# A transformer encoder layer on one core: the order of work at its start, in its routing stage and at its end

## The chip, the cores and the metric

One core of a Trainium2 chip runs the whole layer as one program, float32 throughout except for small bfloat16 index and mask tables. The metric is the device time of one execution in microseconds. The kernel before takes 2204.61 us (median of 3 runs, 2203.73 to 2205.79). Engines: TensorE (PE, its weight loads PEld), VectorE (DVE), ScalarE (ACT), GpSimd (POOL), SyncE (SP), which only issues DMAs.

## The reference, cut to what matters

1024 tokens of width 1024, one layer, in float32:

```
h    = rmsnorm(x, norm1);  proj = h @ w_in            # 1024 x 2048: q, k, v, pool
att  = diff_attention(q, k, v, rel_table, lambda)     # 4 heads, T5 bias by distance
pool = pool_mixer(p, w_pool, pool_scale)              # windows 2, 4, 8, 16
x    = x + concat(att, pool) @ w_out
h    = rmsnorm(x, norm2);  logits = h @ w_router + b_router
topv, topi = top_k(logits, 4);  gates = softmax(topv)  # 4 of 32 experts
# each expert on its own tokens:
#   g = min(h@w_gate+b_gate, 7);  u = clip(h@w_up+b_up, -7, 7)
#   y = ((u+1) * g * sigmoid(1.702 g)) @ w_down + b_down, times its gate
out  = rmsnorm(x + sum of the gated y, final_norm)
```

rmsnorm scales each token by the inverse root of the mean of its squares, then by a gain per channel.

## The kernel before, in words

The code holds one instruction stream per engine, written out by hand; semaphores are the only order between them, and within an engine or a DMA queue everything goes in program order. A DMA adds 16 to its semaphore. Tokens are in eight tiles of 128.

**Start (0 to 220 us).** SyncE loads token tiles 0 to 3, the pool columns of `w_in` (8 loads of 256 KB, semaphores `s_w[k]`), the q, k, v columns (8 loads of 768 KB, one semaphore `s_wqkv`, L457), the relative-bias table, its one-hot matrix and the edge factors (L460, `s_small`), four lambda vectors, and token tiles 4 to 7 (L464). For each tile ScalarE sums the squares (`square_tokens`, L775), GpSimd makes the inverse root (L583, L584), VectorE scales the tile (`scale_tokens`, L1015) into one of two buffers, TensorE transposes it in eight 128x128 blocks (`transposes`, L1413), and VectorE moves them with the gain into `hT` (`move_hT`, L1021, two moves a tile). The projection is done by a Winograd form of Strassen's scheme in eight column pairs: `half_product` multiplies half of the inner dimension (4 steps k) of one block. `first_products(n)` makes the two first products of pair n from tokens 0 to 511 (tiles 0 to 3) (L1427; from pair 6 on L1423). ScalarE moves the first (`move_first`, L780), VectorE adds the second (`sum_first`, L1029). Pairs 0 and 1 run interleaved by k, each product 512 tokens wide. Then come four small products that make the bias rows of the heads (L1449), which VectorE moves out of PSUM bank 0 (`bias_and_lambda`, L995, ahead of the factor lambda, L999 to L1005, of which ScalarE makes the exponential, L787); ScalarE stores them (L789) and SyncE repeats them in DRAM. TensorE goes on with pairs 2 to 7; after pairs 3 and 4 it transposes tiles 4, 5 and 6, 7. Those of tile 4 also wait for the bias rows to have left bank 0. A program record of a float32 product is two MATMUL records in the trace.

**Attention and output projection (220 to 505 us)** are not touched. Expert 0's `w_gate` is loaded meanwhile.

**Routing (to 545 us).** Over turns i, software-pipelined: VectorE adds the residual of tile i, normalises tile i-1, scales the gates of tile i-3 (`finish_gates`, L1169, L1170) and finds the top 4 of tile i-2 (`top_k`, L1153 to L1164); ScalarE squares, stores normed rows to DRAM (`store_rows`, L853), takes the exponential of the gates of i-3 (`gate_exp`, L868), moves the router's parts of i-2 (`move_logits`, L874) and the transposes of i-1 (`move_h2T`, L863). TensorE then ranks tokens per expert (L1622); VectorE finds the slots, compares (L1223) and builds the tables of work items (L1250 to L1279). An item is up to 128 tokens of one expert. GpSimd gathers an item's rows from DRAM (`gather_rows`, L685) after all normed rows are stored. TensorE finds row numbers (`first_rows`, L1638), transposes gathered rows (`row_transposes`, L1656), and makes the index products (L1649). Expert 0's `w_up` (L493, waits for the stored normed rows) and `w_down` (L500, waits for the first gather) are loaded by SyncE.

**Items (to 2187 us).** For each item: gate and up products (L1717, L1730), activation, transposes (L1738), down products (L1765, L1776, L1788, L1800). The rows of item j+1 are gathered while j runs. Results are added to DRAM rows by indirect DMAs (L729). The weights of the next expert are loaded as TensorE has used the last.

**End.** During the last item the residual rows come back; ScalarE sums their squares (`square_rows`, L928), GpSimd makes the inverse roots for tiles 0 and 1, 2 and 3, then 4 to 7 at once (L748, L749), VectorE scales them (L1372), SyncE stores them. Then VectorE takes up the last item's result (L1378), whose rows are normed and scattered to the output by themselves (to L756).

Of the kernel before, what the change touches and what calls it, by code (L numbers as in the profile page):

```python
# [30 lines left out]
P = 128  # L31
# [33 lines left out]
def encoder_kernel(nc, t, out):  # L65

    with ExitStack() as ctx:
# [181 lines left out]
        s_wqkv = sem("w_qkv_in")  # L249
        s_grows = sem("gain_rows_in")  # L250
        s_small = sem("small_in")
        s_ident = sem("ident_ready")
# [13 lines left out]
        s_xs = sem("xs_ready")  # L266
        s_xtr = sem("xs_transposed")
# [99 lines left out]
        s_one = sem("last_item_one_ready")  # L367
# [81 lines left out]
        def _(sp):  # L449
# [6 lines left out]
            for k in range(DT):  # L456
                sp.dma_start(w_qkv[:, k, :], wd[k][:, 0:3 * HALF]).then_inc(s_wqkv, 16)  # L457
# [108 lines left out]
        def _(pl):  # L566
            step = [0]

            def link(ins):
# [6 lines left out]
                             pattern=[[-1, P]], channel_multiplier=1).then_inc(s_ident, 1)  # L576
# [3 lines left out]
            pl.wait_ge(s_const, 3)  # L580
# [11 lines left out]
            def weight_sums(n):  # L592
# [5 lines left out]
                if n == 2:  # L598
                    pl.wait_ge(s_wqkv, 16 * DT)
# [140 lines left out]
            pl.memset(lsq[:, UNIT:UNIT + 1], 1.0).then_inc(s_one, 1)  # L740
# [5 lines left out]
            for lo, hi in ((0, 2), (2, 4), (4, 8)):  # L746
# [16 lines left out]
        def _(act):  # L763
# [18 lines left out]
            for i in range(4):  # L782
                square_tokens(i)
            for n in range(2):
                move_first(n)
            act.wait_ge(s_lamd, 2)
            act.activation(lame, lamd, ACT.Exp).then_inc(s_lame, 1)  # L787
            act.wait_ge(s_bvec, 4)
            act.dma_start(bvec_d[:, :], bvec).then_inc(s_bvout, 16)  # L789
            for i in range(4, TT):  # L790
                square_tokens(i)
            act.wait_ge(s_bps, 4)
            for n in range(2, PAIRS):
                move_first(n)
# [81 lines left out]
            for i in range(TT + 2):  # L876
# [101 lines left out]
        def _(dve):  # L978
# [13 lines left out]
            def bias_and_lambda():  # L992
                for c in range(4):
                    dve.wait_ge(s_bps, c + 1)
                    dve.tensor_copy(bvec[:, c * HALF:(c + 1) * HALF],  # L995
                                    PS[32 * c:32 * c + HEADS, 0:HALF]).then_inc(s_bvec, 1)
                dve.wait_ge(s_lamin, 64)
# [197 lines left out]
            for i in range(TT + 2):  # L1195
# [820 lines left out]
```

## Time and profile before

| what | value |
|---|---|
| median of 3 runs | 2204.61 us |
| profiled execution, its own time | 2207.8 us |
| its span | 2206.0 us |
| TensorE busy | 2133.9 us (97%) |
| VectorE, ScalarE, GpSimd busy | 676.1, 615.0, 506.0 us |
| mean granted TensorE clock | 0.985 of full |
| DMA | 500.71 MB, mean 227 GB/s |

TensorE does nearly all that lies on the chain. Of the forty slices of the page the granted clock is 9 tenths or more in all but one, which holds the routing stage (7 tenths).

### The profile page before, as it was taken

Reading aid. Unit: us, or ns where it says so; the run is one execution under the profiler, and the core shown is the slowest. Engines: PE = TensorE matmul, PEld = TensorE weight load, DVE = VectorE, ACT = ScalarE, POOL = GpSimd, SP = SyncE. Lnnn points to the kernel's source line nnn. Section 1 sums busy time; section 2 is a strip of 40 time slices with the busy share of each in tenths; the row PEclk is TensorE's granted clock in tenths of the full one; section 3 lists DMA queues with packets and bytes.
Section 4 is the critical chain, followed back from the end, with each engine's and each line's share of the span. In section 5 each row is a group of like instructions: output and inputs, shape, how many; then the busy total and the mean of one; then the engine's idle time right before and its main releaser. Section 6 shows DMA issues by size and latency. Waiting matters only on the chain.

```text
span 2206.0 us, 30272 instructions
## 1 busy us (share of the span) xinstructions
PE 2133.9 (97%) x10160; PEld 997.1 (45%) x10161; DVE 676.1 (31%) x1911; ACT 615.0 (28%) x1200; POOL 506.0 (23%) x519
## 2 busy tenths in 40 slices
PE   7999999996999999999998999999999999999996
PEld 3547676543444344344343434434443444444443
DVE  3322898245231221211222212212112211222123
ACT  2000887112222332222223222222222222222223
POOL 3172112123211222121122121221112121222222
PEclk9999999997999999999999999999999999999998
DMA  8000200425758878668869696794889868677775
GB/s 313 0 36 7 111 1 2 154 99 223 245 170 330 295 256 270 251 239 293 329 231 352 233 347 214 242 324 151 330 312 370 338 241 291 240 255 266 260 267 190
DMA packets 150746, 500.71 MB, mean 227 GB/s; under 512 B 10553, under 2 KB 35918, under 8 KB 150158
## 3 DMA queue, kind: packets, MB, share of 16 engines
q1 hardware_dynamic: 115040, 444.81, 52.6%
q0 software_dynamic: 33792, 50.35, 11.1%
q10 hardware_dynamic: 1874, 5.02, 0.6%
q8 instruction: 24, 0.39, 0.1%
q14 instruction: 16, 0.13, 0.0%
HBM read 461.26 MB, written 43.09 MB: 229 GB/s over the span
## 4 chain that ended last, share of the span: by engine, by line
PE 93%; DMA 4%; DVE 1%; issue 1%; SPq 1%; ACT 0%; POOL 0%; DVEq 0%; ACTq 0%; POOLq 0%
PE psum L1730 42%; PE psum L1765 14%; PE psum L1427 6%; PE psum L1528 5%; PE psum L1776 5%; PE psum L1551 3%; PE psum L1517 3%; PE psum L1423 2%; PE psum L1656 2%; PE psum L1717 2%; DMA weights<-in_w_down 2%; PE psum L1738 2%; PE psum L1800 1%; PE psum L1788 1%; PE psum L1560 1%; DMA weights<-in_w_up 1%
## 5 line engine op out<-in xcount | busy, mean ns | idle before, releaser
L1730 PE MATMUL psum<-weights,work 128*128 128x512 f32 (+2 forms) x3008 | 950.1, 595 | 3.4 <-DMA weights<-in_w_up 3.4
L1730 PEld LDWEIGHTS psum<-weights,work 128*128 128x128 f32 (+2 forms) x3008 | 366.7, 159 | 518.8 <-issue 517.5
L729 POOL DMA_INDIRECT residual_rows<-work x184 | 286.8, 1559 | 530.7 <-ACT work L947 480.0
L1765 PE MATMUL psum<-weights,work 128*128 128x512 f32 x768 | 337.5, 592 | 0.0
L1240 DVE SCALAR_TENSOR_TENSOR work<-psum,work 128x4 f32<-128x4 f32 x47 | 7.6, 163 | 841.7 <-PE psum L1649 841.7
L685 POOL DMA_INDIRECT work<-normed_rows,work x48 | 55.3, 1152 | 755.8 <-PE psum L1656 581.3
L1765 PEld LDWEIGHTS psum<-weights,work 128*128 128x128 f32 x768 | 142.2, 190 | 160.7 <-issue 160.7
L917 ACT ACTIVATE work<-psum 128x256 f32<-128x256 f32 x188 | 72.0, 383 | 420.2 <-PE psum L1730 391.6
L1306 DVE TENSOR_SCALAR work<-psum 128x256 f32<-128x256 f32 x188 | 79.8, 424 | 291.3 <-ACT work L917 291.1
L947 ACT ACTIVATE work<-psum,work 128x256 f32<-128x256 f32 x184 | 72.2, 475 | 321.5 <-PE psum L1765 229.5
L897 ACT ACTIVATE work<-psum 128x512 f32<-128x512 f32 x96 | 57.6, 600 | 342.4 <-PE psum L1656 341.9
L1528 PE MATMUL psum<-weights 128*128 128x512 f32 x256 | 112.7, 594 | 0.0
L1776 PE MATMUL psum<-weights,work 128*64 128x512 f32 x480 | 109.6, 598 | 0.0
L1427 PE MATMUL psum<-weights 128*128 128x512 f32 x240 | 107.8, 606 | 1.3 <-DVE weights L1021 1.3
L921 ACT ACTIVATE work<-psum 128x256 f32<-128x256 f32 x188 | 72.5, 386 | 129.5 <-PE psum L1738 129.5
L1311 DVE SCALAR_TENSOR_TENSOR work<-work 128x256 f32<-128x256 f32 x188 | 80.0, 426 | 19.5
L1105 DVE CUSTOM_DVE_ANT_0 work<-psum,weights 128x1024 f32<-128x1024 f32 x64 | 78.4, 1225 | 11.6 <-PE psum L1517 11.4
L812 ACT ACTIVATE work<-work,negmax 128x1024 f32<-128x1024 f32 x64 | 73.3, 1145 | 22.2 <-DVE negmax L1109 22.2
L1308 DVE TENSOR_TENSOR work<-psum,work 128x256 f32<-128x256 f32 x188 | 78.0, 415 | 0.0
L1427 PEld LDWEIGHTS psum<-weights 128*128 128x128 f32 x240 | 46.4, 195 | 60.1 <-issue 58.6
L1717 PE MATMUL psum<-weights,work 128*32 128x256 f32 x1024 | 64.1, 407 | 8.2 <-DMA weights<-in_w_up 6.7
L1528 PEld LDWEIGHTS psum<-weights 128*128 128x128 f32 x256 | 47.4, 190 | 54.1 <-issue 54.1
(236 smaller groups left out, 1856.3 us busy)
## 6 DMA issues: line engine op xcount, KB each, us to landing
weights<-in_w_gate SPq DMA_DIRECT2D x64, 2048.0 KB, 7.9
weights<-in_w_up SPq DMA_DIRECT2D x64, 2048.0 KB, 12.5
weights<-in_w_down SPq DMA_DIRECT2D x64, 2048.0 KB, 11.4
weights<-in_w_in SPq DMA_DIRECT2D x8, 768.0 KB, 14.2
residual_rows<-x SPq DMA_DIRECT2D x9, 512.0 KB, 3.8
normed_rows<-work ACTq DMA_DIRECT2D x9, 512.0 KB, 3.9
x<-in_x SPq DMA_DIRECT2D x8, 512.0 KB, 9.6
bias_rows_repeated<-bias_rows SPq DMA_DIRECT2D x4, 1024.0 KB, 9.8
```

Of the source, the lines that this page charges most:

```text
L729: pl.indirect_dma_start(acc_d[:, :], bass.IndirectOffsetOnAxis(dest[:, b:b + 1], 0), yrow[:, b * BLK:(b + 1) * BLK], None, compute_op=ALU. ...
L812: act.activation(pr, pr, ACT.Exp, bias=negmax[:, c:c + 1], accum_out=expsum[:, c:c + 1]).then_inc(s_ex, 1)
L1105: dve.tensor_tensor_reduce(out=prob[:, set_of(u), m, :], in0=PS[:, 2 * m * HALF:(2 * m + 2) * HALF], in1=bias[:, h, at:at + SEQ], scale=1. ...
L1306: dve.tensor_scalar(ucl[:, b, :], bank(b, BLK, BLK), LIMIT + 1.0, 1.0 - LIMIT, ALU.min, ALU.max).then_inc(s_ucl, 1)
L1308: dve.tensor_tensor(gact[:, b, :], bank(b, BLK), sig[:, b, :], ALU.mult).then_inc(s_sg, 1)
L1311: dve.scalar_tensor_tensor(hid[:, b, :], gact[:, b, :], ACT_LIMIT, ucl[:, b, :], ALU.min, ALU.mult).then_inc(s_hid, 1)
L1427: mm = pe.matmul(bank(b), w[:, k, :], a[:, k, :], start=k == 0, stop=k == 3)
L1528: mm = pe.matmul(bank(n % 4), mixT[:, c, i * P:(i + 1) * P], w_out[:, c, q * HALF:(q + 1) * HALF], start=(c == 0), stop=(c == DT - 1))
L1717: mm = pe.matmul(out, xT[:, k, 0:32], wgu[:, :, k, at:at + P], start=(k == 0), stop=(k == DT - 1))
L1730: mm = pe.matmul(out.rearrange("p (m n) -> p m n", m=2), xT[:, k, lo:lo + cols], wgu[:, :, k, blk * BLK:(blk + 1) * BLK], start=(k == 0), ...
L1765: mm = pe.matmul(bank(4 + h), actT[:, k, :], wdn[:, k, h * HALF:(h + 1) * HALF], start=False, stop=(k == DT - 1))
L1776: mm = pe.matmul(PS[64 * h:64 * h + 64, 4 * HALF:5 * HALF], actT[:, 2 * b + s, 64 * c:64 * c + 64], wdn[:, k, h * HALF:(h + 1) * HALF], st ...
```

## The change

Four places, told in the order of the streams.

1. Start. `w_qkv`'s second four loads get their own semaphore, and pair 2's second product waits for it. ScalarE scales tiles 2 and 3 with the inverse root. TensorE's first products of pairs 0 and 1 run on token columns 0 to 255 (tiles 0, 1) and then on 256 to 511; tile 3 is transposed after step k=1. The bias-row products come after pair 2. ScalarE squares tiles 4 to 7 right after moving pairs 0 and 1. VectorE scales tiles 4 and 5, makes the factor, sums pair 2, and then moves the bias rows.
2. Routing. Order of ScalarE's and VectorE's last turns; SyncE's loads of `w_up` and `w_down` of expert 0 no longer wait for the stored rows and the gather; TensorE transposes the gathered rows ahead of its register loads and the second `first_rows`.
3. End. Inverse roots in pairs of tiles.
4. Two semaphores are merged into others.

```diff
 # SyncE
-                sp.dma_start(w_qkv[:, k, :], wd[k][:, 0:3 * HALF]).then_inc(s_wqkv, 16)
+                sp.dma_start(w_qkv[:, k, :], wd[k][:, 0:3 * HALF]).then_inc(s_wqkv if k < 4 else s_wqkv_hi, 16)
             sp.wait_ge(s_y1, 2 * TT)
-            for b in range(2):
-                sp.wait_ge(s_xnout[b], 16 * TT // 2 + 16 * (1 - b))
             for half in range(2):
                 load_gu(1, half, 0)
-            sp.wait_ge(s_xg, 16)
             for half in range(2):
                 load_dn(half, 0)
 # GpSimd
-            pl.memset(lsq[:, UNIT:UNIT + 1], 1.0).then_inc(s_one, 1)
+            pl.memset(lsq[:, UNIT:UNIT + 1], 1.0).then_inc(s_lsq, 1)
-            for lo, hi in ((0, 2), (2, 4), (4, 8)):
+            for lo, hi in ((0, 2), (2, 4), (4, 6), (6, 8)):
 # ScalarE, start
             for i in range(4):
                 square_tokens(i)
+            for i in range(2, 4):
+                act.wait_ge(s_rstd, i + 1)
+                act.wait_ge(s_xtr, 2 * i - 2)
+                act.activation(xs[:, i % 2, :], xv[:, i, :], ACT.Copy, scale=rstd[:, i:i + 1]).then_inc(s_xs_act, 1)
             for n in range(2):
                 move_first(n)
+            for i in range(4, TT):
+                square_tokens(i)
             act.wait_ge(s_lamd, 2)
             act.activation(lame, lamd, ACT.Exp).then_inc(s_lame, 1)
+            move_first(2)
             act.wait_ge(s_bvec, 4)
             act.dma_start(bvec_d[:, :], bvec).then_inc(s_bvout, 16)
-            for i in range(4, TT):
-                square_tokens(i)
             act.wait_ge(s_bps, 4)
-            for n in range(2, PAIRS):
+            for n in range(3, PAIRS):
                 move_first(n)
 # ScalarE, routing
-                if i >= 3:
+                if 3 <= i < TT:
                     gate_exp(i - 3)
                 if i >= 2:
                     move_logits(i - 2)
                 if 1 <= i <= TT:
                     move_h2T(i - 1)
+                if i >= TT:
+                    gate_exp(i - 3)
 # VectorE, start (bias_and_lambda is split into move_bias_rows and difference_factor)
             scale_tokens(0)
+            scale_tokens(1)
             for i in range(4):
-                if i < 3:
-                    scale_tokens(i + 1)
                 move_hT(i)
             sum_first(0)
             sum_first(1)
-            bias_and_lambda()
-            sum_first(2)
             scale_tokens(4)
             scale_tokens(5)
+            difference_factor()
+            sum_first(2)
+            move_bias_rows()
             sum_first(3)
 # VectorE, routing
-                if i >= 3:
+                if 3 <= i < TT:
                     finish_gates(i - 3)
                 if i >= 2:
                     top_k(i - 2)
+                if i == TT:
+                    finish_gates(TT - 3)
...
             compare(pick0)
+            finish_gates(TT - 2)
             finish_gates(TT - 1)
 # TensorE, start
-            for i in range(4):
+            for i in range(3):
                 transposes(i)
-            pe.wait_ge(s_hT, 8)
-            for k in range(DT):
-                pe.wait_ge(s_w[k], 16)
-                for n in range(2):
-                    mm = half_product(n, ("A11", "A12")[k // 4], ("B11", "B21")[k // 4], 4 + 2 * n + k // 4, ks=[k % 4])
-                    if k % 4 == 3:
-                        mm.then_inc(s_proj, 1)
-            pe.wait_ge(s_small, 16 * N_SMALL)
-            for c in range(4):
-                pe.matmul(PS[32 * c:32 * c + HEADS, 0:HALF], reltab, onehot[:, c * HALF:(c + 1) * HALF],
-                          start=True, stop=True).then_inc(s_bps, 1)
-            pe.wait_ge(s_wqkv, 16 * DT)
+            for half in range(2):
+                pe.wait_ge(s_hT, 4 * half + 4)
+                for k in range(DT):
+                    if half == 0:
+                        pe.wait_ge(s_w[k], 16)
+                    for n in range(2):
+                        mm = half_product(n, ("A11", "A12")[k // 4], ("B11", "B21")[k // 4], 4 + 2 * n + k // 4, [k % 4],
+                                          slice(half * 2 * P, (half + 1) * 2 * P))
+                        if half == 1 and k % 4 == 3:
+                            mm.then_inc(s_proj, 1)
+                    if half == 0 and k == 1:
+                        transposes(3)
             for n in range(2, PAIRS):
+                if n == 2:
+                    pe.wait_ge(s_wqkv, 16 * 4)
                 first_products(n)      # its second product waits for s_wqkv_hi when n == 2
+                if n == 2:
+                    pe.wait_ge(s_small, 16 * N_SMALL)
+                    for c in range(4):
+                        pe.matmul(PS[32 * c:32 * c + HEADS, 0:HALF], reltab, onehot[:, c * HALF:(c + 1) * HALF],
+                                  start=True, stop=True).then_inc(s_bps, 1)
 # TensorE, routing, after the product of the item tables
+            pe.wait_ge(s_xg, 16)
+            row_transposes(0)
             pe.wait_ge(s_tab, 3)
             second = pe.value_load(items[0:1, 1:2], min_val=0, max_val=EXPERTS - 1)
             n_items = pe.value_load(total[0:1, 0:1], min_val=EXPERTS, max_val=MAX_ITEMS)
-            pe.wait_ge(s_xg, 16)
-            row_transposes(0)
-            first_rows(1, bass.ds(second, 1), pickT, second_rows_out)
-            pe.wait_ge(s_xT, 1)
-            row_transposes(1)
-            pe.wait_ge(s_parts, TT)
...
+            # the register loads of the first item, before behind index(1), now stand here
+            pe.wait_ge(s_xT, 1)
+            row_transposes(1)
+            first_rows(1, bass.ds(second, 1), pickT, second_rows_out)
+            pe.wait_ge(s_parts, TT)
```

## Rows read from the trace of the kernel before

**Rows 1.** The page's part 4, first line: share of each engine.
```profile
PE 93%; DMA 4%; DVE 1%; issue 1%; SPq 1%; ACT 0%; POOL 0%; DVEq 0%; ACTq 0%; POOLq 0%
```

**Rows 2.** Timeline to 100 us: start, duration, engine, line, operation, count [idle before <-releaser].
```profile
8.23 4.85 PE L1413 MATMUL psum<-ident,work 128*128 128x128 f32 x24 [1.12 <-DVE work L1015]
...
15.89 14.00 PE L1427 MATMUL psum<-weights 128*128 128x512 f32 x32 [1.30 <-DVE weights L1021]
...
21.04 6.51 SPq L464 DMA_DIRECT2D x<-in_x  x4
...
32.40 1.47 PE L1449 MATMUL psum<-work 32*4 32x512 f32 x8 [2.50 <-DMA edge<-in_edges]
...
33.80 16.91 PE L1427 MATMUL psum<-weights 128*128 128x512 f32 x32
33.87 2.83 DVE L995 COPY work<-psum 4x512 f32<-4x512 f32 x4 [3.18 <-PE psum L1449]
...
41.12 1.06 ACT L775 ACTIVATE work<-x 128x1024 f32<-128x1024 f32 x1
...
67.78 13.98 PE L1423 MATMUL psum<-weights 128*128 128x256 f32 x64
```

**Rows 3.** One source line's transfers, from issue to landing: L457, then L464.
```profile
DMA to landing us min/median/max: 9.6/14.2/19.9
...
DMA to landing us min/median/max: 12.1/12.6/13.2
```

**Rows 4.** Stretches, start and attention: length, busy of five engines, PEclk, DMA share, GB/s.
```profile
30.00:32.00 2.00, 0.00 (x0) 0.00 (x0) 0.69 (x1) 0.00 (x0) 0.00 (x0) 1.00 1.01 166
...
39.00:40.00 1.00, 1.00 (x3) 0.51 (x2) 0.00 (x0) 0.91 (x3) 0.58 (x2) 0.65 0.00 0
...
230.00:235.00 5.00, 3.33 (x17) 1.54 (x16) 3.84 (x7) 4.12 (x9) 0.00 (x0) 1.00 1.02 410
```

**Rows 5.** Timeline of the routing stage, 512 to 550 us.
```profile
512.73 0.94 SPq L493 DMA_DIRECT2D weights<-in_w_up  x2
...
512.79 0.19 DVE L1153 TENSOR_TENSOR work<-psum,work 128x32 f32<-128x32 f32 x1
...
515.90 0.19 DVE L1153 TENSOR_TENSOR work<-psum,work 128x32 f32<-128x32 f32 x1 [0.43 <-PE psum L1597]
...
522.40 1.23 POOL L685 DMA_INDIRECT work<-normed_rows,work  x1 [3.89 <-issue]
...
528.14 0.92 SPq L500 DMA_DIRECT2D weights<-in_w_down  x2
...
529.66 1.11 PE L1656 MATMUL psum<-ident,work 128*128 128x128 f32 x4 [2.30 <-issue]
...
534.19 0.98 POOL L685 DMA_INDIRECT work<-normed_rows,work  x1 [4.34 <-PE psum L1656]
...
535.34 4.97 PE L1717 MATMUL psum<-weights,work 128*32 128x256 f32 x64 [1.51 <-issue]
...
543.23 0.65 PE L1656 MATMUL psum<-ident,work 128*128 128x128 f32 x4 [2.93 <-DMA work<-normed_rows,work]
...
544.59 5.35 PE L1717 MATMUL psum<-weights,work 128*32 128x256 f32 x64
```

**Rows 6.** Source line L685 (gathers of an item's rows), issue to landing.
```profile
DMA to landing us min/median/max: 4.2/7.8/8.9
```

**Rows 7.** Timeline of the last items and the end.
```profile
2134.53 3.66 PE L1717 MATMUL psum<-weights,work 128*32 128x256 f32 x64
...
2177.44 10.46 PE L1765 MATMUL psum<-weights,work 128*128 128x512 f32 x24
2177.62 0.69 POOL L749 TENSOR_TENSOR weights<-weights,halfneg 128x2 f32<-128x2 f32 x1
...
2182.86 0.20 POOL L748 TENSOR_SCALAR weights<-weights 128x4 f32<-128x4 f32 x1 [4.55 <-ACT weights L928]
...
2184.26 4.87 DVE L1372 SCALAR_TENSOR_TENSOR x<-x,weights,work 128x1024 f32<-128x1024 f32 x4 [3.43 <-POOL weights L749]
```

More of the change, by code:

```diff
@@ L266, in encoder_kernel @@
         s_xs = sem("xs_ready")
+        s_xs_act = sem("xs_ready_act")
         s_xtr = sem("xs_transposed")
@@ L579, in _ @@
             pl.memset(pT[:, :, PAD + SEQ:], 0.0).then_inc(s_const, 1)
-            pl.wait_ge(s_const, 3)
+            pl.wait_ge(s_const, 4)
             def rsqrt_mean(dst, src, n, scratch):
@@ L598, in weight_sums @@
                 if n == 2:
-                    pl.wait_ge(s_wqkv, 16 * DT)
+                    pl.wait_ge(s_wqkv, 16 * 4)
+                    pl.wait_ge(s_wqkv_hi, 16 * 4)
                 if n >= 2:
@@ L996, in bias_and_lambda, with difference_factor @@
                                     PS[32 * c:32 * c + HEADS, 0:HALF]).then_inc(s_bvec, 1)
+            def difference_factor():
                 dve.wait_ge(s_lamin, 64)
@@ L1394, in _ @@
         def _(pe):
-            pe.wait_ge(s_ident, 1)
+            pe.wait_ge(s_const, 4)
             pe.wait_ge(s_grows, 64)
@@ L1401, in transposes @@
             def transposes(i):
-                pe.wait_ge(s_xs, i + 1)
+                if 2 <= i < 4:
+                    pe.wait_ge(s_xs_act, i - 1)
+                else:
+                    pe.wait_ge(s_xs, i + 1 if i < 2 else i - 1)
                 if i == 0:
@@ L1414, in transposes, with half_product @@
                     mm.then_inc(s_xtr, 1)
-            def half_product(n, tokens, weights, b, ks=range(4)):
+            def half_product(n, tokens, weights, b, ks=range(4), cols=slice(0, HALF)):
                 a, w = tok_blk[tokens], wgt_blk(n, weights)
@@ L1426, in half_product @@
                 for k in ks:
-                    mm = pe.matmul(bank(b), w[:, k, :], a[:, k, :], start=k == 0, stop=k == 3)
+                    mm = pe.matmul(bank(b)[:, cols], w[:, k, :], a[:, k, cols], start=k == 0, stop=k == 3)
                 return mm
@@ L1433, in first_products @@
                 half_product(n, "A11", "B11", 4 + 2 * (n % 2)).then_inc(s_proj, 1)
+                if n == 2:
+                    pe.wait_ge(s_wqkv_hi, 16 * 4)
                 if n >= 2:
@@ L1667, in _ @@
             n_items = pe.value_load(total[0:1, 0:1], min_val=EXPERTS, max_val=MAX_ITEMS)
-            pe.wait_ge(s_xg, 16)
-            row_transposes(0)
-            first_rows(1, bass.ds(second, 1), pickT, second_rows_out)
-            pe.wait_ge(s_xT, 1)
-            row_transposes(1)
-            pe.wait_ge(s_parts, TT)
-            pe.wait_ge(s_sel, 1)
-            pe.wait_ge(s_idx, 1)
-            index(0, parts_e[:, 0, :, :], pick0)
-            index(1, at=4)
             next_tokens = pe.alloc_register("next_tokens")
@@ L1685, in _ @@
             pe.reg_load(third_expert, items[0:1, 2:3])
+            pe.wait_ge(s_xT, 1)
+            row_transposes(1)
+            first_rows(1, bass.ds(second, 1), pickT, second_rows_out)
+            pe.wait_ge(s_parts, TT)
+            pe.wait_ge(s_sel, 1)
+            pe.wait_ge(s_idx, 1)
+            index(0, parts_e[:, 0, :, :], pick0)
+            index(1, at=4)
             def rows_of(b):
@@ L1956, in _ @@
             pe.wait_ge(s_glast, 32)
[L1957 to L1958 removed]
+            pe.wait_ge(s_lsq, 1 + UNIT)
             for n, lhs in enumerate((ident[:, :], same[:, 0, :], same[:, 1, :])):
```

10 lines of the change are left out of this document (4 added, 6 removed).

## The prediction

> **What bounds the kernel now.** Page first: TensorE is busy 97% of the span, and of the chain that ended last 93% is its work [rows 1], so time is to be had only where TensorE stands still, runs at the lower clock, or has ended. I read the clock slices of the page, TensorE's waits, and then the timelines of the three places that the diff touches. The reader is to see:
>
> Start. TensorE transposes three token tiles until 13.08 us, waits for the fourth and its move, and starts the first products only at 15.89; they end at 29.9; it stands 2.5 us for a small transfer, does the bias-row products, and goes on at 33.8 [rows 2]. These 2.5 us cost more: the granted clock, full (2.4 GHz) at 30 to 32 us, falls to half behind the hole and rises only within 39 to 40, where the mean is 0.65 [rows 4], so the next 32 records (pairs 2 and 3) take 16.91 us where the first 32 took 14.00 [rows 2].
>
> Routing, 505 to 545 us. A chain on VectorE with short steps of the others; TensorE is idle or at the lower clock; the last wait is the second gather of rows, 534.19 to 543.1 [rows 5].
>
> End. TensorE's last product streams to 2187.9, but VectorE takes it up only at 2189.1, since its four last row scalings began at 2184.26, after one wait for four square sums [rows 7].
>
> Between these, TensorE has no wait that the diff touches: an earlier start is passed on one to one. The three stalls on expert weights later are of loads that TensorE's own progress releases, so they move along.
>
> **Start.** The order becomes: transposes of tiles 0, 1, 2; products on token columns 0 to 255 with the transposes of tile 3 after k=1; columns 256 to 511; pair 2; bias-row products; pair 3; and so on.
> Scaling of tiles 2 and 3 goes from VectorE (0.75 us each) to ScalarE (about 1.1, as its squares of the same 128x1024). ScalarE ends its fourth square at 10.4 and so delivers tile 2 at 11.5, as VectorE did. The third tile's transposes still end near 13.0 (they are the last 8 of the first 24 [rows 2]). VectorE has one scaling less ahead of its moves of tile 1, which then end near 12.4. Products start at 13.0 in place of 15.9.
> Weights: the eight small loads land 7.6 to 8.3 us after issue, the last at 15; k=7 is wanted at 19.8: no wait. Each product is cut in two of half width: 64 records in place of 32. The records of 256 columns in a later stretch (64 in 13.98 us [rows 2]) take 0.218 us each; the 128x128 weight loads take 0.19 and hide. So 14.0 us of products plus 0.9 us for tile 3's eight transposes: end at 27.8.
> Pair 2, first product: 8 records, 3.4 us, to 31.2. It needs the first four of the large loads, issued until 9.4 and landed by 23 (median 14.2 us after issue). The other four end with the last at 10.99+19.9=30.9 [rows 3]: no wait, or tenths. Second product to 34.6. Bias rows: their last input was there at 32.4 [rows 2]; 1.47 us at half clock, 0.8 at full: 35.4. Pair 3: 6.9 us, to 42.3, against 50.7 before. That would be 8.4 us.
> It is not all kept, because of what now stands before the next transposes: they wait for the four moved bias rows (same PSUM bank). VectorE moves these after the difference factor and the sum of pair 2; the factor waits for ScalarE's exponential, which is now queued behind the squares of tiles 4 to 7. Tile 7's load is the fourth at 21.04 and after, issued about 26.9, landing 12.1 later = 39.0 [rows 2, 3]. Square (1.06 [rows 2]) with its read, 1.25: 40.3; exponential and factor 0.7: 41.0; sum of pair 2: 41.8; four moves 2.83 [rows 2]: 44.7. TensorE stands 2.4 us and does the transposes at 44.8 in place of 50.6: gain 5.8 us. The bias rows' store lands near 47 instead of 39; its first reader is VectorE's first token sum, over 20 us behind the store before, and the loads made from it are wanted far later still.
> Does this stall drop the clock? Bounds: 1.67 us of idle in 230 to 235 left it at 1.00 [rows 4]; the 2.5 us at 30 dropped it, for 16.91-13.8=3.1 us, and the 2.9 us before 543.2 did too, for 5.35-3.66=1.7 [rows 5, 7]. In those places little but idle surrounds it or small products follow; here full-size products stand on both sides. I take no drop, gain 5.8; bounds 2.7 and 8.4.
> The merged semaphores (identity, the constant one), the split weight wait and GpSimd's order of waits cost nothing: each was signalled microseconds before its reader.
>
> **Routing.** In the last two turns the move of logits and of transposed rows goes ahead of the gates' exponentials, and VectorE's top-4 ahead of the gate scalings. Before, tile 6's logits waited on ScalarE for an exponential that waited for tile 5's top-4; VectorE then stood until 512.79 [rows 5]. Now they are moved near 510.1; top-4 of tile 6 starts when that of tile 5 ends (511.8) and takes 1.9, to 513.7. One gate scaling (0.4), then tile 7's at 514.1 against 515.90 [rows 5]: 1.8 us. After the first comparison there are now two gate scalings, 0.4 more, of which 0.1 to 0.2 falls into VectorE's wait for the row products: 0.3 back. So the tables and both index chains are 1.5 us early.
> The loads: w_up (4 MB) is issued at 507 rather than 512.7 and w_down (4 MB) right behind it rather than at 528.1, when the first gather had landed [rows 5]. At the 0.41 MB/us of the stretch they and the stores fill the DMA engines until about 532. So the first gather, issued at 520.9, meets them all the way. It took 5.7 us before with half its time free; gathers span 4.2 to 8.9 [rows 6], and the one under the w_down load took 8.9. I take 8.2: landed 529.1, against 528.1.
> TensorE's first transposes were held until 529.66 by the register loads behind the tables; now they stand ahead of them: 529.2 to 530.3. Then five register loads instead of two (2 us, from the 1.5 us that two took), the second transposes at 532.4, the second row product to 534.4, the second gather's issue 1.9 later: 536.2, later than 534.19. But the DMA is free by then: 4.4 us, 540.6. TensorE starts item 0's first half near 535.9 (register loads already done; 535.34 before), ends it in 4.97 at 540.8, and goes on at once: 540.8 for 543.2, 2.4 us. With no 2.9 us hole the clock stays up: 64 records in 3.66 instead of 5.35 [rows 5, 7], 1.7. Together 4.1. Bounds: if the first gather takes 5.7 it lands at 526.6, everything is ready 2.4 us sooner: 6.5. If the gather's contention and the moved register loads cost all that the order gives: 0; below that, the rival.
> The normed rows' last store (509.8) has 11 us until the gather needs it; it took 3.
> GpSimd's parts of the gates are done before the first gather as before (518.5), and the four further ones of the last two tiles end at 528, ahead of the second.
>
> What the loads do to a gather shows as 8.9 us in full traffic, 4.2 free. The Trainium skill (DMA: Bandwidth & Descriptors, Queues, rings and completion order) says that each DMA engine alternates between the queues that have work, packet by packet, whichever engine issued it. Worked out from that rule, and so an estimate: the 0.5 MB of a gather would lose only its own length once more, 1.2 us, and land near 526.5; the routing sum by it would be that of rival 2. The 4.7 us between free and full [rows 6] are more than the rule allows, so the trace does not agree, and the sum goes by the rows.
>
> **End.** The square sums of tiles 4, 5 are there at 2180.3 (one square and its read, 1.24 each, before the last two), of 6, 7 at 2182.8. A pair costs GpSimd about 1.1 (0.2, a gap, 0.69 for the power of 128x2), four cost 1.4 [rows 7]. VectorE's tiles 4 and 5 run 2181.5 to 2183.9, tiles 6 and 7 2183.95 to 2186.4: 2.7 us earlier than 2189.1. What is late next is the last product: 2187.9. Gain 1.15 us. Bounds: 0 (were the product's real end later) and 2.7.
>
> **Sum.** 5.8+4.1+1.1=11.0 us. The profiled execution took 2207.8 (span 2206.0); 2196.8. The median shown is 3.2 below it: 2193.6.
>
> **Rivals.**
> 1. The stall at 42 us drops the clock: 1.7 to 3.1 back, 2196.0. For it: a hole of 2.5 did so at 30. Against: 1.67 did not.
> 2. The first gather is as quick as before: 2191.2. For: separate queues. Against: the 8.9.
> 3. Half-width products pay for their weight loads: 32 more loads; if 0.1 to 0.19 us of each shows, the first products end 3 to 6 us later and the 2.4 us stall takes the first of it: 0.6 to 3.6 lost, 2196.5 at 0.165 each. For: a load (0.19) nearly fills the 0.218. Against: that later stretch runs at this pace.
> 4. Routing gives nothing and the clock drops: 2.7+0+1.1=3.8, 2200.8: no change.
> 5. Slower: the 8 MB drain ahead of what is behind them. 8/0.41=20 us from 507: the last normed rows land at 530, the first gather (8.9) at 539, the second is issued near 546 and lands at 550.5 or, at 8.9, 555: 12 us later than 543.1, less 1.7 of clock, less 6.9 of start and end: +3.4; with rival 1 too +5.8, 2210. It decides once the second gather lands later than about 551.7. For: w_down no longer waits for the gather, which looks like a guard. Against: the gather under w_down still took only 8.9.
>
> **Chances.** Forecast 0.40 (own range 2191.5 to 2195.5), rival 1 0.22, rival 2 0.12, rival 3 0.10, rival 4 0.10, rival 5 0.06. About 0.2% (4.4 us) is what a measurement of this kernel tells from none. Faster: 0.84; same 0.10 (rival 4); slower 0.06. Range 2188.5 to 2200.5: from a routing gain of 6.5 with the whole 8.4 of the start to just past rival 4's edge.
>
> **What would show it.** First products from 13.0; second product of pair 2 near 31 without a wait; a wait of TensorE on the moved bias rows of 2 to 3 us near 42 and clock 1.00 behind it (or not: rival 1); tile 7's top-4 at 1.8 us less; first gather landing in 8 us; no hole before the second gather's transposes; last row scaling 2.7 us before its old time. Wrong if TensorE waits for w_in at 16 to 31 us, if the gap at 42 is over 5 us, or if item 0 starts later than before by over 3 us.

## The result and the profile after

The changed kernel takes 2240.3 us (median of 4 runs) against 2204.2 us before (4 runs): ratio 1.0167, 95% interval 1.0149 to 1.0186. It is 36 us slower; forecast were 11 us less. The profiled execution took 2243.7 us, its span is 2241.9.

The page of the changed kernel; of part 3 the last row but one is the queue that brings instructions (number, MB, share). Its part 4 answers to [rows 1]:
```profile
span 2241.9 us, 30339 instructions
...
q8 instruction: 60, 0.98, 0.2%
...
PE 92%; DMA 4%; issue 2%; DVE 1%; SPq 0%; POOL 0%; ACT 0%; DVEq 0%; ACTq 0%; POOLq 0%
...
L1752 PE MATMUL psum<-weights,work 128*128 128x512 f32 (+2 forms) x3008 | 961.2, 602 | 33.8 <-issue 29.9
...
L1739 PE MATMUL psum<-weights,work 128*32 128x256 f32 x1024 | 66.4, 415 | 17.3 <-issue 9.5
```
And the rows of the page before that answer to them, none of which the prediction looked at:
```profile
q8 instruction: 24, 0.39, 0.1%
...
L1730 PE MATMUL psum<-weights,work 128*128 128x512 f32 (+2 forms) x3008 | 950.1, 595 | 3.4 <-DMA weights<-in_w_up 3.4
...
L1717 PE MATMUL psum<-weights,work 128*32 128x256 f32 x1024 | 64.1, 407 | 8.2 <-DMA weights<-in_w_up 6.7
```
L1752 and L1739 are the gate and up products of the items, L1730 and L1717 before; no line of theirs was edited. They now wait 29.9 and 9.5 us on "issue", that is on nothing that the profile shows, and are busy 11.1 and 2.3 us longer. The instruction queue made 60 transfers instead of 24.

**The edited stages did nearly what was forecast.** TensorE's timeline of the start, after, with VectorE's moves of the bias rows (DVE; answers to [rows 2]):
```profile
12.71 1.89 PE L1440 MATMUL psum<-weights 128*128 128x256 f32 x8
...
15.31 15.69 PE L1440 MATMUL psum<-weights 128*128 128x256 f32 x64
...
33.14 3.70 PE L1440 MATMUL psum<-weights 128*128 128x512 f32 x8 [2.15 <-DMA weights<-in_w_in]
36.77 1.04 PE L1474 MATMUL psum<-work 32*4 32x512 f32 x8
37.74 7.13 PE L1440 MATMUL psum<-weights 128*128 128x512 f32 x16
...
42.32 2.82 DVE L1000 COPY work<-psum 4x512 f32<-4x512 f32 x4
...
45.24 1.94 PE L1426 MATMUL psum<-ident,work 128*128 128x128 f32 x16 [0.37 <-issue]
```
First products from 12.71 (forecast 13.0), the next transposes at 45.24 (44.8). But the stall is elsewhere: 2.15 us on `w_in` at 31, and 0.37 instead of 2.4 ahead of those transposes.

Routing, after (answers to [rows 5]):
```profile
515.42 1.22 POOL L683 DMA_INDIRECT work<-normed_rows,work  x1 [1.33 <-issue]
...
523.18 1.12 PE L1678 MATMUL psum<-ident,work 128*128 128x128 f32 x4 [2.80 <-DMA work<-normed_rows,work]
...
528.40 0.98 POOL L683 DMA_INDIRECT work<-normed_rows,work  x1 [5.55 <-DVE work L1242]
529.06 5.64 PE L1739 MATMUL psum<-weights,work 128*32 128x256 f32 x64 [0.75 <-issue]
534.71 0.65 PE L1678 MATMUL psum<-ident,work 128*128 128x128 f32 x4
```
The first gather is used 7.8 us after its issue (8.2 forecast), the second at most 6.3; the hole of 2.93 us before the second transposes is gone. The second item's products begin at 544.70, against 554.87 before: 10.2 us ahead, where 5.8 + 4.1 were forecast. At the end the last product waits for nothing that scales rows (answers to [rows 7]):
```profile
2215.05 10.46 PE L1787 MATMUL psum<-weights,work 128*128 128x512 f32 x24
...
2222.43 2.48 DVE L1382 SCALAR_TENSOR_TENSOR x<-x,weights,work 128x1024 f32<-128x1024 f32 x2 [0.58 <-POOL weights L747]
2225.55 1.66 DVE L1388 SCALAR_TENSOR_TENSOR work<-psum,work,weights 128x256 f32<-128x256 f32 x4 [0.64 <-PE psum L1787]
```

**All of the loss lies in the items.** From the first product of the second item to the start of the last product of all: 1632.4 us before, 1680.2 after, 47.8 more. TensorE's timeline where a 96-token item ends (L1810 is its last line) and a 32-token one begins, after:
```profile
733.15 3.66 PE L1810 MATMUL psum<-weights,work 128*32 128x256 f32 x64
742.44 1.49 PE L1739 MATMUL psum<-weights,work 128*32 128x256 f32 x9 [5.63 <-issue]
747.06 5.43 PE L1739 MATMUL psum<-weights,work 128*32 128x256 f32 x55 [3.14 <-issue]
```
Stretches of it; the columns are those of [rows 4], and the third number from the end is PEclk, the granted share of the full clock:
```profile
730.00:737.00 7.00, 6.81 (x80) 2.84 (x76) 0.23 (x1) 0.88 (x4) 0.00 (x0) 1.00 1.02 413
737.00:750.00 13.00, 4.42 (x37) 2.19 (x41) 0.00 (x0) 3.93 (x6) 6.23 (x4) 0.67 1.05 372
...
742.00:744.00 2.00, 1.49 (x9) 0.56 (x10) 0.00 (x0) 0.00 (x0) 1.69 (x2) 0.50 1.02 406
```
Before, the 64 products there took 3.66 us in one piece; now 9 of them come after a hole of 5.63 us, and the other 55 after one of 3.14. The granted clock is 1.00 until the hole, 0.50 behind it at 742 to 744, and 0.67 on average from 737 to 750.

The kept trace also has the start of each transfer of the instruction queue. Before, the last of the 24 starts at 733.6 us. After, two start in the first of these holes, at 737.1 and 738.9, and one in the second, at 744.8. The changed kernel has eight waits on issue of over 1 us among its items: in seven of them at least one such transfer starts, and the eighth, of 1.79 us, begins as one ends.

### The profile page after: what moved, and what is told of

The parts are those of the page before. It is cut to its first block, busy times and chain, and to the rows that moved or that the text cites. A ratio compares the mean times of both kernels' runs of the same rounds, so it can differ in the third digit from the quotient of the medians.

```text
span 2241.9 us, 30339 instructions
## 1 busy us (share of the span) xinstructions
PE 2141.1 (96%) x10192; PEld 1003.7 (45%) x10193; DVE 673.1 (30%) x1909; ACT 617.0 (28%) x1202; POOL 510.3 (23%) x521
## 4 chain that ended last, share of the span: by engine, by line
PE 92%; DMA 4%; issue 2%; DVE 1%; SPq 0%; POOL 0%; ACT 0%; DVEq 0%; ACTq 0%; POOLq 0%
PE psum L1752 42%; PE psum L1787 15%; PE psum L1440 6%; PE psum L1550 5%; PE psum L1798 4%; PE psum L1573 3%; PE psum L1539 3%; PE psum L1739 2%; PE psum L1436 2%; PE psum L1678 2%; PE psum L1760 2%; DMA weights<-in_w_down 2%; PE psum L1810 1%; PE psum L1822 1%; PE psum L1582 1%
## 5 line engine op out<-in xcount | busy, mean ns | idle before, releaser
L1752 PE MATMUL psum<-weights,work 128*128 128x512 f32 (+2 forms) x3008 | 961.2, 602 | 33.8 <-issue 29.9
L1752 PEld LDWEIGHTS psum<-weights,work 128*128 128x128 f32 (+2 forms) x3008 | 369.6, 161 | 557.4 <-issue 554.3
L1550 PE MATMUL psum<-weights 128*128 128x512 f32 x256 | 112.7, 594 | 0.0
L1798 PE MATMUL psum<-weights,work 128*64 128x512 f32 x480 | 109.6, 598 | 0.0
L1440 PE MATMUL psum<-weights 128*128 128x512 f32 (+1 forms) x272 | 105.3, 543 | 2.1 <-DMA weights<-in_w_in 2.1
L1739 PE MATMUL psum<-weights,work 128*32 128x256 f32 x1024 | 66.4, 415 | 17.3 <-issue 9.5
L1440 PEld LDWEIGHTS psum<-weights 128*128 128x128 f32 x272 | 51.2, 190 | 52.8 <-issue 48.2
L1550 PEld LDWEIGHTS psum<-weights 128*128 128x128 f32 x256 | 47.4, 190 | 54.1 <-issue 54.1
```

The source lines that it names most:

```text
L1440: mm = pe.matmul(bank(b)[:, cols], w[:, k, :], a[:, k, cols], start=k == 0, stop=k == 3)
L1550: mm = pe.matmul(bank(n % 4), mixT[:, c, i * P:(i + 1) * P], w_out[:, c, q * HALF:(q + 1) * HALF], start=(c == 0), stop=(c == DT - 1))
L1739: mm = pe.matmul(out, xT[:, k, 0:32], wgu[:, :, k, at:at + P], start=(k == 0), stop=(k == DT - 1))
L1752: mm = pe.matmul(out.rearrange("p (m n) -> p m n", m=2), xT[:, k, lo:lo + cols], wgu[:, :, k, blk * BLK:(blk + 1) * BLK], start=(k == 0), ...
L1798: mm = pe.matmul(PS[64 * h:64 * h + 64, 4 * HALF:5 * HALF], actT[:, 2 * b + s, 64 * c:64 * c + 64], wdn[:, k, h * HALF:(h + 1) * HALF], st ...
```

## The experiments

**What was suspected.** Cutting the 16 first products in halves adds 16 products, and with one wait TensorE's program is 65 instructions longer ahead of the items' code (counted in the compiled program, where a float32 product is four instructions, two weight loads and two products). By the same count the loop over items with its four bodies, for 32, 128, 64 and 96 tokens, is 1622 instructions, and begins at instruction 4710 before and at 4775 after. In the straight part of the program before, transfers 2 to 18 of the instruction queue (16 KB each) come every 252 product and weight-load records on average, waits and register work not counted: 256 instructions. So the loop is 6.33 such blocks long, and touches seven or, in about 85 of 256 places, eight. The theory of the code's place (theory C where the expectations use letters): in an eight-block place it no longer stays in the engine's instruction memory, and items begin with a fetch. Rivals: the changed start and routing shift transfers so that later ones collide (theory D); or more instructions cost as such. A ratio below is against executions of the kernel before that ran beside the experiment, whose median was 2202.5 to 2206.9 us.

Where TensorE's edited program and an unedited one are told apart, only instructions that never run are added:
```diff
             pe.reg_mov(turn, 0)
-            pe.br("experts_next")
+            pe.br_lt(turn, n_items, on_true="experts_next", on_false="experts_unused")
...
+            with here("experts_unused"):
+                for _ in range(COUNT):
+                    pe.matmul(next_out, parts_next, sel[:, 0:1], start=True, stop=True)
+                pe.br("experts_next")
```
with COUNT 32 (65 instructions), 64 (129), 96 (193) or 16 (33).

**e1, kernel before, 65 unused instructions.** 

> The kernel before with 65 TensorE instructions that never run (32 small products and a branch, jumped over once) between the routing stage and the item code: the item code then starts at instruction 4775 of TensorE's program, where the changed kernel has it, instead of 4710. Theory C (place of the code): the changed kernel's item bodies cover one fetch block more than can be held, so that TensorE waits for code at changes of item kind. Then this kernel too takes 2204 + about 46 = 2245 to 2255 us, with some 60 instruction transfers instead of 24, though nothing it executes has changed. Theory D (transfers: the early loads of w_up and w_down, or the new order of register loads, put the items out of step): within 1 us of 2204, 24 transfers.


Measured: 2251.1 us, ratio 1.0211 (1.0193 to 1.0229). Its waits of TensorE (us in total, times, longest), and its instruction queue:
```profile
PE psum L1730 <- issue: 29.1, 9, 7.3
PE psum L1717 <- issue: 11.0, 3, 6.1
```
```profile
q8 instruction: 56, 0.92, 0.2%
```
Nine and three waits, the same numbers as after (9 of 29.9, 3 of 9.5). Not one edit of the change is in this kernel, so its loss comes with the added instructions or with the place that they give the code; e3 tells these apart.

**e2, changed kernel, 129 unused instructions** (4904). 

> The changed kernel with 129 such unused TensorE instructions at the same place: the item code starts half a block further on. Theory C: no wait for code, 24 to 26 instruction transfers, and the time is 2204 less the 5.3 us gained at the start, 4.9 in routing and about 1.2 at the end: 2192 to 2194 us. Theory D: as the changed kernel, about 2240 us.


Measured: 2194.2 us, ratio to before 0.9956 (0.9940 to 0.9973). The same place in time as the fence above, e2, and its queue:
```profile
733.51 3.66 PE L1810 MATMUL psum<-weights,work 128*32 128x256 f32 x64
737.01 3.66 PE L1739 MATMUL psum<-weights,work 128*32 128x256 f32 x64
```
```profile
q8 instruction: 25, 0.41, 0.1%
```
No hole, 25 transfers, and the items take 1632.4 us as before. More instructions make it fast again.

**e3, kernel before, 193 unused instructions** (4903). 

> Control: the kernel before with 193 unused TensorE instructions, so its item code starts at the same place in a block as in the second run. Theory C: 2204 us within 1, no wait for code: unused code costs nothing where it doesn't add a block. If the unused code by itself cost time (whatever its amount), this would be slower than the first run.


Measured: 2204.1 us, 0.9999 (0.9989 to 1.0008), 25 transfers. The branch and the instructions themselves cost nothing that these runs can tell (0.1%, 2 us): what costs is the place.

**e4, changed kernel with whole products** (4711). Tile 3 is transposed first and the products run on all 512 columns, as before:
```diff
-            for half in range(2):
-                pe.wait_ge(s_hT, 4 * half + 4)
-                for k in range(DT):
...
-                    if half == 0 and k == 1:
-                        transposes(3)
+            transposes(3)
+            pe.wait_ge(s_hT, 8)
+            for k in range(DT):
```


> The changed kernel, but the first products of pairs 0 and 1 run 512 tokens wide after all four tiles, as before; all else as changed. It has 65 fewer TensorE instructions ahead of the items. Theory C: no wait for code; routing and end gains stay (4.9+1.2), of the start's 5.3 some 1 to 3 us are lost or none (the bias rows' wait hides it): 2193 to 2198 us. Theory D: about 2240 us.


Measured: 2195.1 us, 0.9962 (0.9948 to 0.9977), 24 transfers. TensorE's start in e4, then in e2:
```profile
15.72 20.87 PE L1440 MATMUL psum<-weights 128*128 128x512 f32 x48 [0.96 <-DVE weights L1028]
36.52 1.04 PE L1470 MATMUL psum<-work 32*4 32x512 f32 x8
```
```profile
32.24 3.70 PE L1440 MATMUL psum<-weights 128*128 128x512 f32 x8 [1.60 <-DMA weights<-in_w_in]
35.88 1.04 PE L1474 MATMUL psum<-work 32*4 32x512 f32 x8
```
In e4 pair 2 follows in the same row without a wait (48 records); the bias rows come 0.6 us later than in e2 and the next transposes 0.16 later (44.45, 44.29). The headline edit, starting on two tiles, brings nothing that the times show: what it gains in products it gives back waiting for `w_in`. In e4 the first transposes even began 1.4 us later (8.70 against 7.29); from there to the first attention scores e4 takes 204.4 us, e2 205.7 and the changed kernel 206.3, against 209.8 to 212.2 in the kernels whose start is unedited. It is also the edit with 64 of the 65 instructions. What gains the 5 to 6 us of the start is the rest together: bias rows out of the way, ScalarE's scalings and squares, VectorE's order, the two-part wait on the weights. No run tells these apart.

**e9 and e10, where the slow places lie** (4743 and 4839). 

> Kernel before with 33 TensorE instructions that never run (16 small products and a branch) ahead of the item code, which then begins at instruction 4743 of TensorE's program (before 4710, changed 4775). Theory of the code's place: the item code is 6.33 blocks of 256 instructions; where it touches eight blocks it no longer stays in the instruction memory. A stretch of this length touches eight blocks in about a third of all places (84 to 86 of 256 in a row) and seven in the others. The lower edge of the slow places lies above 4710 and at or below 4775, so 4743 is slow only if the edge is at or below it: then 2249 to 2252 us with 56 to 60 instruction transfers, else 2204 with 24 or 25. Nothing between. Rival, that each instruction added costs its share: 2204 + 47 * 33/65 = 2228 us, with some 40 transfers.

> The same with 129 unused instructions: the item code begins at 4839. Theory of the place: it cannot be slow together with 4743, which lies 96 lower, more than the slow stretch is wide; 4839 is slow only if the lower edge is at or above 4755. Then 2249 to 2252 us with 56 to 60 transfers, else 2204 with 25. Rival, that added instructions cost their share: at 193 the cost was gone, so somewhere between; a gradual fall from 65 to 193 gives half of the 47 us, 2228.


Measured: e9 2269.7 us, 1.0303 (1.0279 to 1.0328); e10 2204.9 us, 1.0013 (1.0002 to 1.0023).
```profile
q8 instruction: 86, 1.41, 0.3%
...
```
```profile
q8 instruction: 25, 0.41, 0.1%
...
```
(e9, then e10). The theory allows at most one of the two to be slow, and one is. Nothing grows with the count: half the added instructions of e1 cost more, and twice as many cost 0.4 to 5 us by the interval, not 47. That rival is out. But the expected size was wrong for e9: 67 us and 86 transfers instead of 47 and 60. So within the slow places the price still depends on the place.

**What the waits follow.** In after, e1 and e9 all waits on issue of over 1 us that lie in the items, but one of 1.10 us in e9, begin in the first or second item behind one of 96 tokens. There are eight such items: after and e1 wait behind six of them, e9 behind all eight. In time over the items of before that is, on average, 47.8/6 = 8.0 us, e1 45.9/6 = 7.6 and e9 63.4/8 = 7.9 us each. These three kernels and e12 below have 27 such waits of over 2 us, and in each of them a transfer of the instruction queue is under way. The 96-token body is the last of the code, so by the count above it alone reaches into the eighth block.

**e12, changed kernel, other order of the bodies.**
```diff
-            for tokens in (32, 128, 64, 96):
+            for tokens in (32, 128, 96, 64):
```


> The changed kernel with the four item bodies in the order 32, 128, 96, 64 tokens: same instructions, same length, same place (4775), only the 64-token body is now the last of the code instead of the 96-token one. In the changed kernel and in the two slow shifted ones every wait of TensorE on nothing but issue of 1 us or more begins in the two items that follow an item of 96 tokens (8 such items), at about 8 us in all each. Theory: the eighth block is fetched only when the last body runs, and pushes out the first; so the waits move behind the seven items of 64 tokens (behind each or most of them) and none stays behind an item of 96: 2194 + 5 to 7 times 8 = 2234 to 2250 us. Rival, that it is something in the 96-token body itself (its length, its many short products): the waits stay behind its eight items, some 2240 us. The time hardly tells them apart, the places of the waits do.


Measured: 2223.0 us, 1.0076 (1.0047 to 1.0105), 54 transfers. TensorE where a 64-token item (its down products are L1798) gives way to one of 128:
```profile
607.35 5.37 PE L1798 MATMUL psum<-weights,work 128*64 128x512 f32 x24
615.87 15.69 PE L1752 MATMUL psum<-weights,work 128*128 128x512 f32 x32 [3.15 <-issue]
```
```profile
PE psum L1752 <- issue: 23.8, 4, 9.8
PE psum L1739 <- issue: 0.8, 1, 0.8
```
The four long waits (from 615.87, 1133.44, 1340.97 and 1717.51 on) stand behind four of the seven 64-token items, and none behind one of 96. The rival is out: the waits moved with the place of the body in the code. Of the theory this part holds; the five to seven paying items that it gave do not, and so the time is below its range: only four pay, 28.9/4 = 7.2 us each. Why four of seven here, six of eight there and eight of eight in e9 is open: it depends on which bodies ran before, and no rule of replacement was found that gives these counts.

**The parts of the change alone.** None of these moves the code out of a fast place (24 transfers in each).

e5, only the end:
```diff
-            for lo, hi in ((0, 2), (2, 4), (4, 8)):
+            for lo, hi in ((0, 2), (2, 4), (4, 6), (6, 8)):
```


> The kernel before with only the end's inverse roots in pairs of tiles. Forecast of the prediction: 1.15 us less (the last product at 2187.9 is next), about 2203.3 by the median; item code at its old place, so no wait for code. Rival: 2.7 us less, if the last product is taken up as soon as the row scalings allow; or nothing, if the stored rows (waited for by the last scatter) or the product's real end bound it.


Measured: 0.9997 (0.9988 to 1.0007). In the trace the time from the start of the last product to the end is 17.0 us against 18.7, as in after, e2 and e4: 1.7 us less in these executions. But kernels whose end is unedited show 18.1 to 18.8 us there, so the gain is 1.1 to 1.7, which the runs don't resolve.

e6, only the early loads (SyncE's three waits taken out):
```diff
-            for b in range(2):
-                sp.wait_ge(s_xnout[b], 16 * TT // 2 + 16 * (1 - b))
...
-            sp.wait_ge(s_xg, 16)
```


> The kernel before with only SyncE's waits ahead of w_up and w_down of expert 0 taken back, all orders as before. Theory A (the second gather is the last wait of routing): the first gather takes 7.7 us instead of 5.7, the second 5.9 or less instead of 8.9; the item loop starts 1 to 3 us earlier, and the clock stays up in the first item: 2200 to 2203 us. Rival: the delayed first gather eats it all: 2204 or 1 to 2 us more.


Measured: 0.9980 (0.9970 to 0.9991), some 4 us less, at the upper edge of what its theory A had (1 to 4).

e7, only ScalarE's and VectorE's last turns (the diff's two routing parts). 

> The kernel before with only the last turns' order of ScalarE and VectorE changed (logits and transposed rows ahead of the gates' exponentials, top-4 ahead of the gate scalings). Prediction's step: tables 1.5 us earlier, so 1.5 us less, 2202.7 by a median of 2204.2. Rival: the earlier gathers meet more of the weight loads and it comes out as no change.


Measured: 1.0000 (0.9991 to 1.0010): the 1.5 us are not seen, and the interval, 2 us to each side, doesn't exclude them.

e8, all three routing edits. 

> The kernel before with all three routing edits (early loads, gate order, TensorE's order of transposes and register loads). Seen between the traces of before and after: 4.9 us between the start of attention and the second item. So 2204 less 4.9: 2199.3. If the three only work together, the two single edits sum to clearly less than this.


Measured: 0.9980 (0.9971 to 0.9990), the same as the early loads alone.

e11, e8 without the early loads. 

> Kernel before with two of the routing edits, ScalarE's and VectorE's last turns and TensorE's transposes ahead of its register loads, while w_up and w_down of expert 0 wait for the stored rows and the gather as before. The early loads alone brought 3 us of the stretch from the scores to the second item, the last turns alone 3.5, all together 4. Theory: the orders alone carry it, since the second gather, which ends the stage, meets no load in either case; the stretch is 3 to 5 us shorter than before, 2200 to 2203 us. Rival: without the early loads the second gather meets w_down and takes 9 us again, so the stretch gains 1 us or less.


Measured: 1.0004 (0.9994 to 1.0014). Here the rival was right: the second gather, issued 5.3 us behind `w_down`, again takes 9.6 us until it is used, and the hole is back (e11, then e8, TensorE and the gather):
```profile
533.25 0.98 POOL L685 DMA_INDIRECT work<-normed_rows,work  x1 [5.35 <-DVE work L1237]
...
542.84 0.75 PE L1661 MATMUL psum<-ident,work 128*128 128x128 f32 x4 [2.37 <-DMA work<-normed_rows,work]
...
544.53 4.70 PE L1722 MATMUL psum<-weights,work 128*32 128x256 f32 x64
```
```profile
534.15 0.98 POOL L682 DMA_INDIRECT work<-normed_rows,work  x1 [5.55 <-DVE work L1234]
...
542.46 3.66 PE L1719 MATMUL psum<-weights,work 128*32 128x256 f32 x64
```
In the traces, the stretch from the first attention scores to the second item is 335.6 us before, 332.6 in e6, 332.0 in e7, 331.8 in e8, 335.3 in e11, 332.1 in e2 and 330.5 in e4. Each of these is one execution: the other kernels whose routing is unedited (e1, e3, e5, e9, e10) lie between 334.1 and 336.0, and e7 and e11 differ by 3.3 though the second gather takes 8.9 and 9.6 in them. So what can be said of routing rests on the timed runs: the early loads carry a gain of some 4 us (0.9980 with and without the rest), and of the orders alone the runs show none.

The best version is the change with its item code in a fast place: e2, or e4 without the split, 2194.2 and 2195.1 us, whose intervals overlap. The start's edits did not run alone on the kernel before; what they bring is seen in the traces and as the remainder.

## Why the prediction was wrong

The step that failed is the sentence "Between these, TensorE has no wait that the diff touches: an earlier start is passed on one to one." It weighed waits on semaphores, DMAs and the clock, and took an unedited loop for unchanged. The diff moved that loop by 65 instructions in TensorE's program, and so put its 1622 instructions where they cost 47.8 us. The trace before held the sign to look at: the instruction queue with its 24 transfers, the last at 733.6 us, in the first item that runs the last body, and then none to the end, though the loop runs on for 1450 us. That is a loop that fits, and the question to ask was by how much.

The idle time and the clock carry it: 38 us of additional issue waits (29.9 + 9.5 against 1.5), and 11.1 + 2.3 us more of busy time at the lower clock, 51 together, 3 more than the stretch shows. A line's busy time can't be read more closely than that: L1730 and its like are busy 949.5 to 953.2 us in the kernels with a fast place, at the same stretch within 3 us.

The Trainium skill (Runtime: NRT & Kernel Launch, Instruction fetch mechanics) says that TensorE's instruction memory is a queue of 2048 instructions refilled in blocks of 256, fetched ahead in sequence, and that a taken branch to a target outside the current window of two pages makes the engine wait for a fetch. The runs fit the size: by the count, a loop that touches seven blocks stays, and one that touches eight does not. The same section also says that the memory is only two cache lines; a loop of seven blocks with no transfer in 1450 us, whose bodies branch back over more than two blocks without a wait, speaks against that and against the window of two pages, and the measurement decides. That the memory has eight blocks, of which one is for the block fetched ahead, is argued from page and runs together, not shown by itself. So is where the blocks begin: counted from instruction 0, 4743 and 4775 would be inside seven and 4839 not; all seven places that ran fit if 36 to 67 instructions stand ahead of the counted ones, a number that was fitted and not measured.

The other steps:
- *Start, 5.8 us*: the first attention scores begin 5.3 us earlier after, 6.2 in e2 and 6.1 in e4 (219.2 before, but 217.4 to 219.9 in the kernels with an unedited start). Right in size. One term was mis-sized: the last large load landed 21.8 us after its issue, not 19.9, so TensorE stood 2.15 us at 31 and was through with pair 3 at 44.9, not at 42.3. It cost next to nothing, since the next transposes wait for VectorE's moves, and these ended at 45.1, as worked out (44.7). Most of the 2.4 us of waiting there was spent at 31 instead, and 0.37 was left.
- *Rival 1, a clock drop from the stall at 42*: its condition did not arise, since only 0.37 us of that stall was left. The 2.15 us of idle at 31, a little less than the 2.5 us that dropped the clock before, left it at 1.00 behind it (stretch of the changed kernel, columns as above):
```profile
33.00:37.00 4.00, 3.86 (x12) 1.54 (x16) 0.00 (x0) 0.80 (x1) 0.00 (x0) 1.00 1.01 388
```
- *Rival 3, half-width products*: right pace. 56 records of 256 columns and 8 of 512 in 15.69 us, as 0.218 and 0.43 each give.
- *Routing, 4.1 us*: 4.9 after, 3.6 in e2, 5.1 in e4, each against the one execution of before; the timed runs of e8 give some 4. First gather 7.8 us (8.2), no hole (right). Two terms were off and in part cancel, which is luck. Item 0's products were to start 0.6 us later than before; counted from the first scores they started 1.0 us earlier after and 0.2 in e2. And the first half of item 0 took 5.64 and, in e2, 6.39 us instead of 4.97, since the clock stayed low longer: mean 0.66 and 0.54 from 529 to 535, against 0.73 from 535.3 to 540.3 before. The second gather took up to 6.3, not 4.4, still hidden. Rival 5 did not come near: the first gather was used at 523.2, not at 539 less the start's gain.
- *Rival 2, the first gather as quick as before (5.7 us)*: out, it took 7.8. But the reading that the trace speaks against alternating queues was wrong, since it took landing times for transfer times. By the packets in the traces of before and after, a gather's own 128 packets of 4 KB take 2.3 us (median of 30 gathers) with no load beside them, and 3.0 us (median of 64, at most 4.2) in full traffic, while 118 to 278 load packets start: one or two for each of its own, as alternating queues would have it. Most of the difference lies before its first packet: 1.9 us from the start of the instruction when free, 4.3 us under the loads (medians). What fills that time is not shown.
- *End, 1.15 us*: 1.1 to 1.7 in the traces.
- *Sum*: without the step that failed it nearly stands. Forecast were 11.0 us less; e2 took 0.9956 of the kernel before, 9.7 us less (5.9 to 13.2), and e4 0.9962. That e2's 2194.2 us is so near to the forecast 2193.6 is in part luck: the kernel before ran at 2202.9 beside it, not at 2204.6.

## What to carry to other kernels

A loop with several bodies and branches between them has a size in instruction blocks and a place, and both belong in the sum of every edit ahead of it on the same engine, even of one that never runs. Count the engine's instructions up to the loop and in it, and look at the instruction queue's row: here, transfers that stopped once all bodies had run meant that the loop fitted, and ones that went on came with waits of microseconds at the start of items. Where a loop is near the edge, unused instructions ahead of it are worth trying before any edit of its content, in several amounts, since 33 and 65 were bad here and 129 and 193 were not. Each edit is to be measured in a fast place before it is judged.

## What the runs showed that was not expected

- 33 instructions that never run cost 67 us of 2204 (e9), 65 cost 47 us (e1), 129 at most 5 us (e10), 193 nothing that can be told (e3).
- An item of the last body that is followed by waits costs about 8 us on average. In the changed kernel that is a hole of 5.6 to 7.3 us, with a second one of 3.1 or 1.8 us behind two of them; behind the second of two such items in a row it is only a hole of about 3 us. A lower clock comes on top (32 records of a 128-token item take 15.69 us in e12 and 14.00 in the same item before).
- What pays is not a long body, but whatever runs after the last body of the code; reordering the bodies alone moved the changed kernel from 1.0167 to 1.0076 of the kernel before (2240.3 and 2223.0 us).
- A 0.5 MB gather under both loads took 7.8 us, behind them 6.3 at most, and 9.6 with `w_down` issued 5.3 us ahead of it. Of these, 4.5, 2.6 and 4.3 us went by before its first packet.
